# The down product of the first block's FFN by seven block products of step-wise operands

## The reference, cut to what matters

```python
D_FF = 2816                       # 22 tiles of 128
h = rms_norm(x, g_ffn[l])
x = x + (jax.nn.silu(h @ w_gate[l]) * (h @ w_up[l])) @ w_down[l]
```

## Time and profile before

| | us |
|---|---|
| median of three runs | 3378.96 |
| the profiled execution, its own time | 3382.82 |
| its span | 3381.0 |
| granted TensorE clock, mean of full speed | 0.973 |

### The profile page before, as it was taken

The page is one execution under the profiler, slowest core; times in us unless marked ns, Lnnn a source line. Parts: engine busy times, 40 slices in busy tenths (PEclk is TensorE's granted clock), DMA queues, the critical chain, the costliest instruction groups (busy, mean ns, idle before and its releaser), DMA issues.

```text
span 3381.0 us, 51779 instructions
## 1 busy us (share of the span) xinstructions
PE 3221.2 (95%) x20325; PEld 2842.4 (84%) x20325; DVE 1654.6 (49%) x2795; ACT 1128.0 (33%) x2100; POOL 990.7 (29%) x672
## 2 busy tenths in 40 slices
PE   7999989899999998999999899999999999789997
PEld 5677767688888877999999799998999999689997
DVE  4555556755554545666666623255455043522223
ACT  3433333333322213555555621155455111300002
POOL 3112223777772333222222133200000222012221
PEclk9999989999999998999999999999999999789998
DMA  4011112112224112000000012100000221468988
GB/s 155 26 32 32 32 63 100 63 64 86 75 98 189 45 48 89 20 26 20 20 20 20 14 44 82 66 24 26 24 22 20 76 88 62 176 220 308 318 306 292
DMA packets 80577, 294.90 MB, mean 87 GB/s; under 512 B 11298, under 2 KB 16226, under 8 KB 77200
## 3 DMA queue, kind: packets, MB, share of 16 engines
q1 hardware_dynamic: 67584, 244.05, 20.6%
q10 hardware_dynamic: 6656, 29.77, 2.2%
q0 software_dynamic: 6160, 18.63, 2.2%
HBM read 239.39 MB, written 47.70 MB: 85 GB/s over the span
## 4 chain that ended last, share of the span: by engine, by line
PE 54%; DVE 3%; issue 2%; ACT 1%; DMA 1%; POOL 0%; SPq 0%; POOLq 0%; DVEq 0%; ACTq 0%
PE PS L630 14%; PE PS L3018 7%; PE PS L3440 6%; PE PS L618 5%; PE PS L3203 4%; PE PS L3470 3%; PE PS L3082 3%; PE PS L3049 3%; PE PS L3279 3%; PE PS L3244 2%; DMA w_down_sb<-in_w_down 0%; PE PS L3083 0%; PE PS L3031 0%; PE PS L3216 0%; DVE where L2870 0%
## 5 line engine op out<-in xcount | busy, mean ns | idle before, releaser
L652 POOL CAST w_hi<-ring 128x1024 fp32r<-128x1024 f32 x130 | 136.8, 1052 | 1550.3 <-PE PS L630 436.9
L654 POOL TENSOR_TENSOR w_lo<-ring,w_hi 128x1024 fp32r<-128x1024 f32 x130 | 332.5, 2558 | 10.5
L2157 ACT ACTIVATE EA<-EA,small_sb 128x1040 f32<-128x1040 f32 x144 | 166.8, 1158 | 192.4 <-DVE small_sb L2560 192.2
L2560 DVE CUSTOM_DVE_ANT_0 EA<-PS,biasH,low_a 128x1024 f32<-128x1024 f32 x128 | 163.6, 1278 | 57.4 <-PE PS L3049 57.4
L3018 PE MATMUL PS<-u_hi,w_hi 128*128 128x348 f32 x504 | 173.6, 345 | 0.0
L3018 PE MATMUL PS<-u_lo,w_hi 128*128 128x348 f32 x504 | 162.2, 322 | 0.0
L3018 PE MATMUL PS<-u_hi,w_lo 128*128 128x348 f32 x504 | 162.0, 321 | 0.0
L1574 DVE TENSOR_TENSOR hid_lo<-hid,hid_hi 128x1024 fp32r<-128x1024 f32 x44 | 92.7, 2145 | 118.7 <-ACT hid_hi L1220 118.7
L1658 PE MATMUL PS<-u_hi,w_hi 128*128 128x512 f32 x352 | 146.9, 417 | 3.0 <-POOL w_lo L654 2.3
L1852 PE MATMUL PS<-t_hi,slot_hi 128*128 128x512 f32 x352 | 138.8, 394 | 9.4 <-DVE t_lo L1473 8.8
L3082 PE MATMUL PS<-Va,PTa 128*128 128x128 f32 (+1 forms) x1152 | 139.9, 275 | 0.0
(11 more groups left out here) (479 smaller groups left out, 8274.4 us busy)
## 6 DMA issues: line engine op xcount, KB each, us to landing
ring<-in_stream SPq DMA_DIRECT2D x130, 512.0 KB, 3.5
w_gate_sb<-in_w_gate SPq DMA_DIRECT2D x64, 512.0 KB, 6.6
w_up_sb<-in_w_up SPq DMA_DIRECT2D x64, 512.0 KB, 7.0
w_down_sb<-in_w_down SPq DMA_DIRECT2D x64, 512.0 KB, 5.4
gu_raw<-in_gate_up SPq DMA_DIRECT2D x22, 1024.0 KB, 5.6
hid_keep<-hid_out SPq DMA_DIRECT2D x17, 512.0 KB, 2.9
hid<-hid_keep ACTq DMA_DIRECT2D x15, 512.0 KB, 16.5
x_keep<-xT ACTq DMA_DIRECT2D x1, 4176.0 KB, 13.1
```

Of the source, the lines that this page charges most:

```text
L652: pool.tensor_copy(w_hi[j][:, :, :], w_raw[j][:, :, :]).then_inc(S["w_rounded"], 1)
L654: pool.tensor_tensor(w_lo[j][:, :, :], w_raw[j][:, :, :], w_hi[j][:, :, :], ALU.subtract).then_inc(S["w_split"], 1)
L2157: act.activation(e[0:m, :], e[0:m, :], ACT.Exp, scale=-1.0, bias=small[0:m, 8 + 2 * par + k:9 + 2 * par + k], accum_out=small[0:m, 12 + 2 ...
L2560: dve.tensor_tensor_reduce(e[0:m, 0:T1], wide(2 * k, T1, m), bias, -1.0, low_a[0:m, t, k:k + 1], ALU.add, ALU.min, low).then_inc(S["aa_max ...
```

## The change

The down product is made by seven block products too. The 2816 FFN rows are cut in halves of 11 inner tiles, the 1024 tokens in halves (B11, B12, B21, B22 of `hid`) and the 1024 output rows in halves (A11, A12, A21, A22 of `w_down`). In order, with the sums each needs:

| product | weight | value | result goes to |
|---|---|---|---|
| 1 | A11 | B11 | all four quarters of x |
| 2 | A12 | B21 | one |
| 3 | S3 = A11 - A21 | T3 = B22 - B12 | two |
| 4 | S1 = A21 + A22 | T1 = B12 - B11 | two |
| 5 | S2 = S1 - A11 | T2 = B22 - T1 | three |
| 6 | S4 = A12 - S2 | B22 | one |
| 7 | A22 | T4 = T2 - B21 | one (subtracted) |

Each product runs over 11 steps k of four row tiles p by three matmuls, so 77 steps of 12 matmuls, 924 in all. The operands are made anew in every step, with four slots: for step q ACT rounds a weight and a value (128x512 each), POOL takes the low weight, DVE the low value. The sums S1, S2, S4 are POOL's, S3 and T1 to T4 DVE's, each 128x512 a step. A product's results are added to x by DVE during the next one (steps k = 3, 5, 7, 9), so two products share the eight banks. Weights come as 99 loads of 256 KB through 12 buffers in `ring`. In the last product the last four steps run row tile by row tile. The splits of `A0` and `A0 + 1` stand within the last product, and DVE waits for the loaded x ahead of the second product's first step. All of it is written out without loops. The diff, cut to its core (added lines; the functions they replace are printed above):

```diff
+DOWN = (("A11", "B11"), ("A12", "B21"), ("S3", "T3"), ("S1", "T1"), ("S2", "T2"), ("S4", "B22"), ("A22", "T4"))
+RAW_SLOTS = 12
+STEP_SLOTS = 4
+TWIST = 4
+DP1, DP2, DP7, DP5, DP6, DP3, DP4 = range(7)
+ADDS = (2, 1, 1, 1, 2, 1, 1)
...
+                def load_down(n):
+                    q, name, k = RAWS[n]
+                    if n >= RAW_SLOTS:
+                        sp.wait_ge(S["dw_lo"], RAWS[n - RAW_SLOTS][0] + 1)
...
-                stream(DOWN0 + 2, TILES + 2)
-                sp.wait_ge(S["w_used"], tile_done(TILES - 1))
+                for n in range(4, len(RAWS)):
+                    load_down(n)
+                sp.wait_ge(S["dw_lo"], DP4 * KH)
+                for j in range(2):
+                    load(sp, A0 + j, j)
+                sp.wait_ge(S["dn_ev"], added(DP4))
...
+                for q in range(DSTEPS):
+                    if q + 1 < DSTEPS:
+                        combine_down(q + 1)
+                    pool.wait_ge(S["dw_hi"], q + 1)
+                    pool.tensor_tensor(d_lo[q % STEP_SLOTS][:, :], weight_source(q), d_hi[q % STEP_SLOTS][:, :], ALU.subtract).then_inc(S["dw_lo"], 1)
+                    if q == DP4 * KH + 2:
+                        pool.wait_ge(S["dw_lo"], DP4 * KH + 1)
+                        split(pool, A0, 0, A0 // 2 + 1, A0 - 2)
+                    if q == DP4 * KH + 6:
+                        split(pool, A0 + 1, 1, A0 // 2 + 1, A0 - 1)
...
+                def round_weight(q):
+                    name = DOWN[q // KH][0]
+                    if q >= STEP_SLOTS:
+                        act.wait_ge(S["dn_used"], q - STEP_SLOTS + 1)
...
+                    act.activation(d_hi[q % STEP_SLOTS][:, :], weight_source(q), ACT.Copy).then_inc(S["dw_hi"], 1)
...
+                round_weight(0)
+                for q in range(2):
+                    round_values(q)
                 silu_half(NF - 1, 1)
+                act.wait_ge(S["gs_used"], used(NF - 1, S4))
+                round_weight(1)
                 act.wait_ge(S["gs_used"], used(NF - 1, A22))
                 act.dma_start(x2T[:, :, :], x_keep).then_inc(S["keep_ld"], 16)
+                round_weight(2)
+                act.wait_ge(S["gs_out"], out_of(NF - 1, "c11"))
+                round_values(2)
...
+                for q in range(STEP_SLOTS, DSTEPS):
+                    if q == STAY.stop:
+                        act.wait_ge(S["hid_ld"], 16 * (NF - 1 - STAY.stop))
+                    round_weight(q)
+                    round_values(q)
...
+                for q in range(2, DSTEPS):
+                    if q == KH:
+                        dve.wait_ge(S["keep_ld"], 32)
+                    s, k = divmod(q, KH)
+                    rest_values(q)
+                    if q + 1 < DSTEPS:
+                        combine_weights(q + 1)
+                    combine_values(s, k)
+                    p, late = divmod(k - 3, 2)
+                    if s and p >= 0 and not late:
+                        add_product(s - 1, p)
...
+                for q in range(DSTEPS - TWIST):
+                    operands_ready(q)
+                    for p in range(HALF):
+                        last = down_step(q // KH, q % KH, p)
+                    last.then_inc(S["dn_used"], 1)
+                operands_ready(DSTEPS - 1)
+                for p in range(HALF):
+                    for k in range(KH - TWIST, KH):
+                        last = down_step(DP4, k, p)
+                last.then_inc(S["dn_used"], 1)
```

More of the change, by code:

```diff
@@ L44 @@
 UP0 = W_OUT0 + KD
[L45 to L46 removed]
+TILES = UP0
 OUT_ORDER = [c for q in range(HALF) for c in (q, HALF + q)]
@@ L474, in build @@
         S.update(first_sems)
+        dw_lds = [nc.alloc_semaphore(name=f"dw_ld{j}") for j in range(RAW_SLOTS)]
         xin_lds = [sem(f"xin_ld{j}") for j in range(NT)]
@@ L854, in _ @@
                     if i == NF - 2:
-                        for j in range(2):
-                            load(sp, DOWN0 + j, j)
+                        for n in range(4):
+                            load_down(n)
                     if i not in STAY and i < NF - 1:
@@ L1214, in _ @@
                 silu_half(NF - 1, 0)
[L1216 to L1220, removed]
+                def round_weight(q):
+                    name = DOWN[q // KH][0]
+                    if q >= STEP_SLOTS:
+                        act.wait_ge(S["dn_used"], q - STEP_SLOTS + 1)
+                    if name in ("S1", "S2", "S4"):
+                        act.wait_ge(S["dw_sum"], q - DP5 * KH + 1)
+                    elif name == "S3":
+                        act.wait_ge(S["dw_diff"], q % KH + 1)
+                    else:
+                        wait_raw(act, q, name)
+                    act.activation(d_hi[q % STEP_SLOTS][:, :], weight_source(q), ACT.Copy).then_inc(S["dw_hi"], 1)
@@ L1233, in _ @@
[L1233 to L1250, removed]
+                round_weight(2)
+                act.wait_ge(S["gs_out"], out_of(NF - 1, "c11"))
+                round_values(2)
+                round_weight(3)
+                round_values(3)
+                act.wait_ge(S["gs_out"], out_of(NF - 1, "hid0"))
@@ L1592, in _, with first_rests @@
                 first_sums(NF - 1)
                 up_right(NF - 1)
-                gates(NF - 1, lambda: rest_tile(0, 0))
+                def first_rests():
+                    for q in range(2):
+                        rest_values(q)
+                gates(NF - 1, first_rests)
                 products(NF - 1, hid[:, NF - 1, :])
[L1596 to L1611, removed]
+                for k in range(2):
+                    combine_values(DP1, k)
@@ L1865, in _ @@
                         product(i, s)
[L1867 to L1875, removed]
-                        if first and not o and k == 0 and d:
-                            pe.wait_ge(S["gs_out"], out_of(NF - 1, ("w", "c11", "c21")[d - 1]))
-                        for q, (w, src) in enumerate(((w_hi, hid_hi), (w_hi, hid_lo), (w_lo, hid_hi))):
-                            for b in range(2):
-                                last = mm(bank(down_bank(d) + b), w[slot][:, k * HALF + d, :], src[2 * slot + k][:, b * BANK:(b + 1) * BANK],
-                                          start=(first and k == 0 and q == 0), stop=(end and k == 1 and q == 2))
-                        if end and k == 1 and d < HALF - 1:
-                            last.then_inc(S["dn_z"], 1)
-                    last.then_inc(S["w_used"], 1)
@@ new lines, in down_step @@
+                def down_step(s, k, p):
+                    j = (s * KH + k) % STEP_SLOTS
+                    if k == 0:
+                        if s == 0 and p:
+                            pe.wait_ge(S["gs_out"], out_of(NF - 1, "w"))
+                        if s >= 2:
+                            pe.wait_ge(S["dn_ev"], added(s - 2, p))
+                    for q, (w, src) in enumerate(((d_hi, o_hi), (d_hi, o_lo), (d_lo, o_hi))):
+                        last = mm(down_bank(s, p), w[j][:, p * P:(p + 1) * P], src[j][:, :], start=(k == 0 and q == 0), stop=(k == KH - 1 and q == 2))
+                    if k == KH - 1 and p < HALF - 1:
+                        last.then_inc(S["dn_p"], 1)
+                    return last
@@ L3524, in layout @@
     late += [*w_in2[GB:GB + KD], *w_b, *w_out2]
-    out["stream"] = np.concatenate([np.stack(tiles), down, np.stack(late)])
+    out["stream"] = np.concatenate([np.stack(tiles), np.stack(late)])
     for n in ("w_gate_2", "w_up_2"):
```

184 lines of the change are left out of this document (134 added, 50 removed).

## The result

The changed kernel takes 3383.5 us (median of 12 runs, 3381.6 to 3386.47), the kernel before, on the same chip, 3376.54 (12 runs): a ratio of 1.0018, 95% interval [1.0011, 1.0025]. It is slower by some 7 us, more than the noise, since the interval leaves out 1, and about the 0.2% that the prediction took as what can be told, where 10.9 less was forecast. The profiled execution took 3386.0 with a span of 3384.2, 3.2 above the span before, at a mean granted clock of 0.972. The spans differ by less than the medians because the profiled execution before lies 6.3 above the median of its kernel's 12 runs and the one after 2.5; and among the ten profiles of this document the time ahead of the stage differs by up to 3.2 us and the time behind its sums of squares by up to 5.1, so what follows goes by the stage itself.

The account below looks back on a forecast made before the run. PE, busy 95% of the span, was taken as the bound, with POOL and DVE turns bounding products 4 to 6. -28.8 + 2.9 + 12.9 + 0.5 + 4.1 - 2.5 = -10.9 us: 3378.96 becomes 3368.1, range 3354 to 3391.

Parts of the forecast that it names:

- Matmuls: Down stage: 1056 matmuls at 0.2270 us become 924 at 0.2282, a step of 12 taking 2.74 us: -28.8 us.
- product 3 rebuilds about 0.4 a step: Product 3: operand making gains about 0.4 us a step on PE, rebuilding lead for product 4.
- 2.30 us for products 1 to 3: Products 1 to 3: one POOL and two DVE passes a step, 1.70 + 0.6 us, under PE's 2.74.
- the lead of 4: Start of product 4: operands ready ahead, 5.6 us at most, taken as 4 against the waits of products 4 to 6.
- First steps: Start of down: PE waits for operands, +2.1 us at step 1 and +0.8 at step 2, sum +2.9, bounds 0 and 5.
- let one POOL pass by: Step 2: DVE's three passes at 0.6 us meet only one POOL pass, so PE waits +0.8 us.
- Late data: `hid` at step 6, x at step 11 and later weights arrive in time: 0 us, bound +1 for `hid`.
- Products 4, 5 and 6: POOL and DVE take turns: 3.40 us a step in products 4 and 5, 2.96 in 6; +12.9 us after the lead.
- Rival 3: Products 4 to 6: turns cost whole spans, 3.94 us a step in 4 and 5; 15.2 us more, 3383.3; chance 0.20.
- Rival 4: Products 4 and 5: PE's short waits drop the clock to 1.2 GHz for half the steps; 3391.0 us; chance 0.12.
- Product 7 and its last steps: Product 7: splits and low parts +0.5 us; before its last four steps a 2.6 us bubble and 1.5 of clock, +4.1.
- Tail: Last addition to sums of squares: 3.25 us in place of 5.73 with the splits gone, -2.5, bounds -2.0 and -3.0.

Follow-up runs that it names:

- Experiment 1: Changed kernel with DVE making product 3's weight difference S3 two steps ahead, not one: 3374.66 us, ratio 0.9988 to the kernel before.
- Experiment 5: Changed kernel with weight 1 rounded ahead of the last sigmoid pass and T1's differences made from step 6 on: 3382.5 us, ratio 1.0017 to the kernel before.
- experiment 2: Changed kernel with both splits of the next weights behind POOL's last low part, not amid product 7: 3379.7 us, ratio 1.0004 to the kernel before.
- experiment 6: As experiment 2, but the last three steps, not four, run row tile by row tile: 3378.85 us, ratio 1.0000 to the kernel before.
- experiment 8: As experiment 7, with T1's differences one a step in steps 4 to 14 and T4 made in product 6: 3354.82 us, ratio 0.9929 to the kernel before.
- experiment 7: Changed kernel with the edits of experiment 1, Experiment 5 and experiment 6, and sums S1, S2, S4 on DVE: 3358.79 us, ratio 0.9941 to the kernel before.

## Why the prediction was wrong

The stage took 15.0 us more than forecast: by the first table 4.8 in product 1, -0.2 in product 2, 4.4 in product 3, 3.9 in products 4 to 6, 1.9 in product 7 (with the rounding, 0.2 less than the whole). By the medians the forecast is off by 17.9, 7.0 for -10.9; the 3 us beyond the stage lie outside it and its tail, and no run shows where.

- **Matmuls**: right. An undisturbed step is 2.72 for the 2.74 assumed.
- **The step that failed** is "product 3 rebuilds about 0.4 a step", with the 2.30 us for products 1 to 3 on which it rests. 2.30 is the sum of the passes that take turns, a throughput; product 3's pace was a latency, 3.25 round the ring of ACT and DVE. So PE lost 4.4 there, and product 4 began without the lead of 4: 8.3 us of the 15.0. The order was in the diff, the next weight difference behind this step's low part in DVE's stream; I priced the instructions and did not follow the order round. Experiment 1 shows it.
- **First steps**: 7.8 over PE's pace, 2.9 forecast. Step 1 was right: it starts 4.4 behind step 0, 1.6 over the pace, for the 2.1 forecast. The clock fell to half in step 0, but that cost nothing, for step 1's operands come no sooner. In experiment 1 the clock stayed at 1.00 there, and PE waited for them until the same 4.4 were over (step 0 starts at 1025.05):

```profile
1029.41 0.47 PE L2030 MATMUL PS<-o_hi,d_hi 128*128 128x512 f32 x1 [1.38 <-POOL d_lo L1012]
```

What failed is "let one POOL pass by", the +0.8 for step 2: all three of DVE's passes took a turn, and PE waited 4.09. Behind that wait the clock was at half for most of step 2 (4.43 us for 2.72), 1.7 more, a term I had only for the end. Experiment 5 shows that the order there sets these waits, and also that winning them alone bought nothing.
- **Late data**: right, nothing. ACT waited for `hid` until 1041.69, and PE came to step 6 at 1049.3; x landed at 1051.4, and no wait of DVE in the stage ends by it:

```profile
1041.69 0.63 ACT L1313 ACTIVATE d_hi<-d_raw 128x512 fp32r<-128x512 f32 x1 [7.82 <-DMA hid<-hid_keep]
```

- **Products 4, 5 and 6**: the turns were right, 3.41 and 2.93 a step for 3.40 and 2.96. Rival 3's whole spans (3.94) were wrong, though its time, 3383.3, is what came out: the sum met the number by other terms. The Trainium skill, "SBUF — State Buffer", Who interferes with whom, has the two engines exclude each other; the runs agree, and put the turn at 1.70, not at the spans' 1.97.
- **Rival 4** was wrong: the clock stayed 1.00 in products 4 to 6 although PE idled 0.4 us in each of 22 steps. The Trainium skill, "TensorE: Matmul & The Clock Gate", A second HAM failure mode, has a clock that swings on short idles between groups of matmuls; these runs do not show it.
- **Product 7 and its last steps**: the bubble was 5.31 for 2.6, since POOL's second split stood ahead of the low parts; I had costed the split as throughput (+0.5) and the bubble as if POOL were free. With the splits behind, it is 2.62. The clock's share was 1.24 (12.11 less 10.87) for 1.5; in experiment 1, behind the same bubble, the last 48 matmuls took 13.53, so it was 2.66 there.
- **Tail**: right. From the last addition, at 1271.67, to PE's 1274.92 it is 3.25, as forecast, against 5.73.

## What to carry to other kernels

Where operands are made step by step by several in-order engines, sum the passes per engine, and of engines that take turns, and then follow one operand round all the engines: if its path comes back to the same engine with one step of lookahead, its latency is the pace, and no engine will look full. Write each engine's order so that what another engine waits for is made one step earlier, and put long work behind, not ahead of, a burst that the critical engine wants at once, and look at what it meets there (2.7 us of bubble won in experiment 2, 1.0 lost in the tail in experiment 6). Where POOL and DVE meet in SBUF, as here, a 128x512 pass moved from POOL to DVE costs 0.6 where it held the pair for 1.16, so the slow engine should keep only what the fast one has no room for; and a lead won in one stretch is worth what the next can spend of it.

## What was not expected of the hardware

The clock fell at the first down step in some kernels and not in others, on almost the same idle time of PE ahead of it. First matmul of down, and the window behind it, in the kernel before, in experiment 8, in the changed kernel and in experiment 7:

```profile
1024.96 0.70 PE L1880 MATMUL PS<-hid_hi,w_hi 128*128 128x512 f32 x2 [1.40 <-DVE hid_lo L1574]
...
1026.00:1028.00 2.00, 2.00 (x11) 1.65 (x10) 1.27 (x3) 0.69 (x2) 0.00 (x0) 1.00 1.03 420
```
```profile
1024.41 0.47 PE L2027 MATMUL PS<-o_hi,d_hi 128*128 128x512 f32 x1 [1.54 <-DVE o_lo L1650]
```
```profile
1025.17 0.48 PE L2030 MATMUL PS<-o_hi,d_hi 128*128 128x512 f32 x1 [1.87 <-DVE o_lo L1672]
...
1026.00:1028.00 2.00, 2.00 (x7) 1.62 (x6) 1.27 (x3) 1.12 (x3) 0.00 (x0) 0.61 1.03 410
```
```profile
1024.80 0.47 PE L2033 MATMUL PS<-o_hi,d_hi 128*128 128x512 f32 x1 [1.96 <-DVE o_lo L1650]
...
1026.00:1028.00 2.00, 2.00 (x6) 1.57 (x6) 1.53 (x3) 0.41 (x1) 0.00 (x0) 0.50 1.05 413
```

After 1.40 and 1.54 us of idle the granted clock stayed at 1.00 (2.4 GHz); after 1.87 and 1.96 it was 0.61 and 0.50 in the window (0.50 is 1.2 GHz, 0.61 a mean of both levels). In the other six profiles it stayed at 1.00 in this step after 1.18, 1.39, 1.45 and 1.45, and fell after 1.82 and 1.93.

The fall looks costly, 4.37 and 4.25 us for step 0 against 2.83 in experiment 8, but in these kernels it cost nothing here. In the changed kernel step 1's operands came no sooner. In experiments 7 and 8 step 2 starts 8.22 and 8.21 us behind step 0: what 7 lost to the clock, 8 waited for step 2's operands, and after its longer wait the clock fell in 8's step 2 (4.44 us) and not in 7's (2.88):

```profile
1033.02 0.50 PE L2033 MATMUL PS<-o_hi,d_hi 128*128 128x512 f32 x1 [0.88 <-DVE o_lo L1650]
...
1033.00:1035.00 2.00, 1.99 (x9) 1.64 (x10) 1.99 (x2) 1.59 (x4) 1.90 (x2) 1.00 1.03 410
```
```profile
1032.62 0.64 PE L2027 MATMUL PS<-o_hi,d_hi 128*128 128x512 f32 x1 [2.50 <-DVE o_lo L1650]
...
1033.00:1035.00 2.00, 2.00 (x6) 1.58 (x5) 1.99 (x3) 1.19 (x3) 2.00 (x2) 0.50 1.05 419
```

So in these steps a fall of the clock was a loss only where PE, and not its operands, bounded the step. That the idle time decides whether it falls was not tried by itself.
